# Probs times v in the column halves of the array, with v as the stationary operand

## The chip, the cores and the metric

The kernel runs on one core of one Trainium2 chip. The metric is the time of one launch on the device, in microseconds (us). The kernel before takes 615.45 us, the median of three runs (615.38 to 615.69).

## The reference

One layer of a hybrid decoder on 512 tokens of 1024 features, all in fp32. What the change touches is the attention of 8 heads of 64 features. With 512 tokens, blocks of 256 keys and a top-k that takes every past block, the block-sparse attention is plain causal attention. Its output is normalised over all 512 features of a token and goes, beside the output of a gated mixer, through the output projection:

```python
def rms_norm(x, g):
    y = xf * lax.rsqrt(jnp.mean(xf * xf, axis=-1, keepdims=True) + NORM_EPS)
...
    s_own = jnp.where(k_pos[None, None, :] <= q_pos[None, :, None], s_own, NEG_INF)
    probs = jax.nn.softmax(jnp.concatenate([s_sel, s_own], axis=-1), axis=-1)
    return (jnp.einsum('hqnl,hqnld->hqd', p_sel, v_sel)
            + jnp.einsum('hql,hld->hqd', p_own, v_own))
...
    mixed = jnp.concatenate([rms_norm(attn_out, attn_out_g[i]),
                             rms_norm(gmlp_out, gmlp_out_g[i])], axis=-1)
    h = h + rms_norm(jnp.einsum('bse,ed->bsd', mixed, w_o[i]), mix_post_g[i])
```

## The kernel before, in words

All matrices go through TensorE (PE). A large product is done as three fp32r matmuls of high and low parts (`product`, lines 1546, 1550, 1551), so every operand is split: ScalarE (ACT) writes the high part, VectorE (DVE) the low part. Tokens come in four tiles of 128. Each engine has its own instruction list, written out by hand; an instruction waits on semaphores, and all behind it on its engine wait with it.

The attention lies in a loop of 16 steps, one for each pair of heads of each tile of queries: `unit = 4 * qt + pair`. In a step PE does

- `scores(step)`: q times k for two heads, head 0 in rows 0 to 63 of the array and head 1 in rows 64 to 127, each into its own PSUM bank;
- `turn_probs(step - 1)`: transposes of the probabilities of the unit before, `qt + 1` for each head;
- `proj(...)`: half a tile of a projection, 4 slabs of weights times 3 matmuls. Steps 0 to 5 do the tiles 17 to 19 (v), steps 6 on those of the output projection (20 to 24);
- `attend(step - 1)`: probs times v (line 1698). The stationary operand is `probsT` (128 keys by 128 queries), the moving one 64 columns of `v`; the result is 128 queries by 64 features per head, so that bank 7 (`BANK_O`) holds attn by tokens. An fp32 matmul shows as two records in the trace: 80 matmuls, 160 records.

When the four pairs of a tile are done (after steps 4, 8, 12 and behind the loop), DVE takes 1/rowsum (line 557, 8 numbers a row) and multiplies it in (559), ACT squares with a sum over the row (924), POOL (GpSimd) makes the rstd (1327, 1328), DVE scales (566), PE turns attn by four transposes (`turn_attn`, in steps 5, 9, 13 behind `attend`), ACT drains the high part into `mixT_hi` and DVE the low part into `mixT_lo` (`attn_turn_hi`, `attn_turn_lo`). The second half of the first output tile of these tokens waits for that: `pe.wait_ge(*drained["attnT", t])`.

On DVE a step is `row_maxima(step)` (mask 536, maximum 541, times minus scale 544; it waits for `scores(step)`), `drain_pt0(step - 1)` (550, half of the transposed probs), then splits of weights in steps 0 to 2 and 5 to 8 (433), and what the attn chain needs. ACT does `drain_pt1` (1028), `softmax` (1019), the high parts of the same splits (890), and its part of the chain. `scores(step)` waits for `softmax(step - 1)`.

Behind the loop PE does `turn_probs(15)`, tile 25, the transposes of the hidden state (`turn_hn`), `turn_attn(3)`, tiles 26 and 27, then eight tiles for the per-layer embedding (`ple_tile`) with `turn_hn(4)` to `(7)` among them, and the MLP.

Of the kernel before, what the change touches and what calls it, by code (L numbers as in the profile page):

```python
# [32 lines left out]
F32 = mybir.dt.float32  # L33
F32R = mybir.dt.float32r
BF16 = mybir.dt.bfloat16
ALU = mybir.AluOpType
# [3 lines left out]
P = 128  # L40
D = 1024
SEQ = 512
TT = SEQ // P
# [70 lines left out]
def phase_one_results():  # L114

    names = []
    for n in range(20):
        names.append(("proj", n))  # L120
        if n in (8, 9):
            names += [("mix", 2 * (n - 8)), ("mix", 2 * (n - 8) + 1)]
        if 9 <= n <= 16:
            names.append(("qkT", n - 9))
        if 12 <= n <= 15:
            names.append(("gateT", n - 12))
    names += [("proj", n) for n in range(20, 26)]
# [6 lines left out]
    late = [(("attnT", 0), b), (("proj", 20), a), (("proj", 21), b), (("attnT", 1), c),  # L134
            (("proj", 22), c), (("proj", 23), a), (("attnT", 2), b), (("proj", 24), b),
            (("hT", 0), 5), (("hT", 1), 6), (("proj", 25), c), (("hT", 2), a), (("hT", 3), 6),
            (("attnT", 3), 5), (("proj", 26), 3), (("proj", 27), 4),
            (("ple", 0), 7), (("ple", 1), 6), (("ple", 2), 5), (("hT", 4), a), (("hT", 5), b),
            (("ple", 3), c), (("ple", 4), 7), (("ple", 5), 6), (("hT", 6), 3),
            (("hT", 7), 4), (("ple", 6), 5), (("ple", 7), a)]  # L140
    banks.update(late)
    return names[:-6] + [name for name, _ in late], banks
# [36 lines left out]
def hymba_layer(nc, x, xT, pT, weights, columns, rope, ws, rows, out):  # L179
# [6 lines left out]
    with ExitStack() as ctx:  # L186
# [34 lines left out]
        rinv = place("rinv", [P, HEADS])  # L221
        ident = place("ident", [P, P])
        ident_bf = place("ident_bf", [P, P], BF16)
        causal = place("causal", [P, P])
        stat = place("stat", [P, 114 + len(GATE_TILES)])
# [52 lines left out]
        minus_half = stat[:, 0:4]  # L278
        ss_x, rstd_x = stat[:, 4:8], stat[:, 8:12]
        ss_gm, rstd_gm = stat[:, 12:16], stat[:, 16:20]  # L280
        ss_at, rstd_at = stat[:, 20:24], stat[:, 24:28]
# [13 lines left out]
        def sem(name):  # L295
# [30 lines left out]
        rinv_ready, attn_ready, at_squared, at_rstd, at_scaled = (  # L326
            sem("rinv_ready"), sem("attn_ready"), sem("at_squared"), sem("at_rstd"), sem("at_scaled"))
# [90 lines left out]
        def _(dve):  # L418
# [134 lines left out]
            def attn_rows(qt):  # L553

                dve.wait_ge(pv_done, PAIRS * (qt + 1))
                sums = rowsum[:, PAIRS * qt:PAIRS * (qt + 1), :].rearrange("p a b -> p (a b)")
                nc.vector.reciprocal(rinv[:], sums).then_inc(rinv_ready, 1)
                dve.wait_ge(rinv_ready, qt + 1)
                nc.vector.tensor_tensor(attn[:].rearrange("p (h d) -> p h d", d=DH),
                                        psum[:, BANK_O, :].rearrange("p (h d) -> p h d", d=DH),  # L560
                                        rinv[:, :, None].to_broadcast([P, HEADS, DH]), ALU.mult
                                        ).then_inc(attn_ready, 1)

            def attn_scale(qt):
                dve.wait_ge(at_rstd, qt + 1)
                nc.vector.tensor_scalar(attn[:], attn[:], rstd_at[:, qt:qt + 1], None, ALU.mult
                                        ).then_inc(at_scaled, 1)

            def attn_turn_lo(qt):
                cut = slice(qt * P, (qt + 1) * P)  # L570
                turn_lo(("attnT", qt), mixT_lo[:, 4:8, cut], mixT_hi[:, 4:8, cut], bank1["attnT", qt])
# [27 lines left out]
            for step in range(TT * PAIRS):  # L599
                if step >= 6 and step % 4 == 2:  # L600
                    attn_turn_lo(step // 4 - 1)
                row_maxima(step)
                if step >= 1:
                    drain_pt0(step - 1)
                if step >= 5 and step % 4 == 1:
                    attn_scale(step // 4 - 1)
                for slab in STEP_SPLITS.get(step, ()):
                    splits(slab)
                if step >= 4 and step % 4 == 0:
                    attn_rows(step // 4 - 1)  # L610
# [4 lines left out]
            drain_pt0(15)  # L615
            hn_turn_lo(0)
            hn_turn_lo(1)
            attn_rows(3)
            attn_scale(3)
            hn_turn_lo(2)  # L620
            hn_turn_lo(3)
            attn_turn_lo(3)
# [256 lines left out]
        def _(act):  # L879
# [150 lines left out]

            def square_attn(qt):
                act.wait_ge(attn_ready, qt + 1)
                square(attn[:], ss_at[:, qt:qt + 1], at_squared)

            def attn_turn_hi(qt):
                turn_hi(filled1["attnT", qt], mixT_hi[:, 4:8, qt * P:(qt + 1) * P], bank1["attnT", qt])
# [8 lines left out]
            def square_h1(t):  # L1045
                act.wait_ge(*drained["proj", 21 + 2 * t])
                square(h[:, t, :], ss_h[:, t:t + 1], h1_squared)
# [16 lines left out]
            for step in range(TT * PAIRS):  # L1064
                if step >= 6 and step % 4 == 2:
                    attn_turn_hi(step // 4 - 1)
                if step >= 1:
                    drain_pt1(step - 1)
                softmax(step)
                for slab in STEP_SPLITS.get(step, ()):  # L1070
# [8 lines left out]
                if step >= 4 and step % 4 == 0:  # L1079
                    square_attn(step // 4 - 1)  # L1080
                if step == 14:
                    square_out(1)
# [4 lines left out]
            norm_h1(1)  # L1087
            square_attn(3)
# [4 lines left out]
            attn_turn_hi(3)  # L1093
# [204 lines left out]
        def _(pool):  # L1298
# [19 lines left out]
            pool.wait_ge(constants_set, 4)  # L1318
# [64 lines left out]
            def attn_rstd(qt):  # L1383
                pool.wait_ge(at_squared, qt + 1)
                rstd(rstd_at[:, qt:qt + 1], ss_at[:, qt:qt + 1], W, at_rstd)

# [5 lines left out]
            def hidden_rstd(t):  # L1392
                pool.wait_ge(h1_squared, t + 1)
                rstd(rstd_h[:, t:t + 1], ss_h[:, t:t + 1], D, h1_rstd)

# [144 lines left out]
        def _(pe):  # L1540
# [33 lines left out]
            def proj(n, k_range=range(KD)):  # L1574
# [17 lines left out]
                if half == 0 and k_range[-1] == KD - 1:  # L1592
                    pe.wait_ge(*drained["attnT", t])
# [37 lines left out]
            def turn_attn(qt):  # L1631
                pe.wait_ge(at_scaled, qt + 1)
                turn(phase1, bank1, ("attnT", qt), attn[:])
# [84 lines left out]
            turn_hn(1)  # L1718
            attend(15)
# [195 lines left out]
```

## Time and profile before

| | before |
|---|---|
| median of 3 runs | 615.45 us |
| the profiled execution | 615.13 us |
| its span | 613.4 us |
| PE busy | 603.8 us, 98% |
| DVE busy | 396.4 us, 65% |
| ACT busy | 311.0 us, 51% |
| POOL busy | 84.2 us, 14% |
| mean granted clock of PE | 0.997 of 2.4 GHz |

The profile is one execution. "Busy" of PE counts matmuls whose ends are modelled and overlap the next one's start; how fast a sequence runs is read from start to start. The attention steps lie between about 112 and 198 us.

### The profile page before, as it was taken

How to read it: one execution, taken by the hardware profiler on the slowest of the kernel's cores; microseconds unless marked ns; L12 is line 12 of the kernel's file. 1: busy time of each engine (PE TensorE's matmuls, PEld its weight loads, DVE VectorE, ACT ScalarE, POOL GpSimd, SP SyncE). 2: the span in 40 equal slices, each digit the busy share in tenths (PEclk: the TensorE clock that was granted, in tenths of full speed). 3: DMA queues.
4: the chain of work that ended last, by engine and by line, in shares of the span. 5: the costliest groups of instructions: out<-in, count | busy, mean ns of one | idle time of the engine just before them, and what ended most of it. 6: DMA issues, size and time to landing. Idle time of an engine off the chain costs nothing.

```text
span 613.4 us, 7770 instructions
## 1 busy us (share of the span) xinstructions
PE 603.8 (98%) x2910; PEld 499.5 (81%) x2910; DVE 396.4 (65%) x587; ACT 311.0 (51%) x541; POOL 84.2 (14%) x155
## 2 busy tenths in 40 slices
PE   8999999999999999999999999999999999999995
PEld 6888888888888888888888888888888888888884
DVE  5476443557545693765867857757668568568654
ACT  6754543655364755554544635545446345534422
POOL 1176332000001120001001001010010010001011
PEclk9999999999999999999999999999999999999998
DMA  8754322223000359564736546637365466234011
GB/s 309 258 189 141 105 103 69 69 69 104 1 2 1 111 202 313 141 218 92 191 138 152 157 138 153 219 79 196 144 128 156 151 154 207 96 130 171 10 70 68
DMA packets 23653, 82.90 MB, mean 135 GB/s; under 512 B 2752, under 2 KB 3136, under 8 KB 23104
## 3 DMA queue, kind: packets, MB, share of 16 engines
q1 hardware_dynamic: 18000, 60.83, 27.8%
q0 software_dynamic: 4032, 14.68, 13.5%
q10 hardware_dynamic: 1584, 6.90, 2.9%
q8 instruction: 23, 0.38, 0.2%
q14 instruction: 14, 0.11, 0.1%
HBM read 78.20 MB, written 4.19 MB: 134 GB/s over the span
## 4 chain that ended last, share of the span: by engine, by line
PE 97%; DMA 1%; DVE 0%; ACT 0%; SPq 0%; POOL 0%; issue 0%; DVEq 0%; ACTq 0%; POOLq 0%
PE psum L1546 30%; PE psum L1551 30%; PE psum L1550 30%; PE psum L1698 3%; PE psum L1600 2%; PE psum L1681 2%; DMA first_raw_a<-weights_dram 1%; PE psum L1614 1%; DVE h L829 0%; SPq L1461 0%; DVE w_lo L433 0%; ACT w_hi L890 0%; POOL stat L1445 0%; DVE acc L811 0%; DVE acc L802 0%
## 5 line engine op out<-in xcount | busy, mean ns | idle before, releaser
L433 DVE SCALAR_TENSOR_TENSOR w_lo<-raw,cols,w_hi 128x512 fp32r<-128x512 f32 x112 | 85.7, 808 | 48.8 <-ACT w_hi L890 48.8
L1551 PE MATMUL psum<-actT_hi,w_lo 128*128 128x512 f32 x256 | 99.8, 390 | 0.0
L1546 PE MATMUL psum<-actT_hi,w_hi 128*128 128x512 f32 x256 | 99.7, 389 | 0.0
L1550 PE MATMUL psum<-actT_lo,w_hi 128*128 128x512 f32 x256 | 99.6, 389 | 0.0
L890 ACT ACTIVATE w_hi<-raw,cols 128x512 fp32r<-128x512 f32 x112 | 74.3, 713 | 42.7 <-PE psum L1546 22.6
L1546 PE MATMUL psum<-w_hi,actT_hi 128*128 128x512 f32 (+1 forms) x232 | 90.7, 391 | 0.8 <-DVE w_lo L433 0.8
L1551 PE MATMUL psum<-w_hi,actT_lo 128*128 128x512 f32 (+1 forms) x232 | 88.9, 383 | 0.0
L1550 PE MATMUL psum<-w_lo,actT_hi 128*128 128x512 f32 (+1 forms) x232 | 88.7, 382 | 0.0
L1551 PE MATMUL psum<-t_hi,a_lo 128*128 128x512 f32 x212 | 83.6, 394 | 0.0
L1546 PE MATMUL psum<-t_hi,a_hi 128*128 128x512 f32 x212 | 83.5, 394 | 0.0
L1550 PE MATMUL psum<-t_lo,a_hi 128*128 128x512 f32 x212 | 83.4, 394 | 0.0
L719 DVE TENSOR_TENSOR acc<-acc,psum 128x512 f32<-128x512 f32 x90 | 58.5, 682 | 23.7 <-PE psum L1551 23.7
L1546 PEld LDWEIGHTS psum<-actT_hi,w_hi 128*128 128x128 f32 x256 | 48.1, 188 | 10.1
L1550 PEld LDWEIGHTS psum<-actT_lo,w_hi 128*128 128x128 f32 x256 | 48.1, 188 | 10.1
L1551 PEld LDWEIGHTS psum<-actT_hi,w_lo 128*128 128x128 f32 x256 | 48.1, 188 | 10.1
L1411 POOL DMA_DIRECT2D raw_x<-weights_dram x21 | 18.6, 885 | 259.1 <-DVE t_lo L660 259.1
L1546 PEld LDWEIGHTS psum<-w_hi,actT_hi 128*128 128x128 f32 x232 | 43.6, 188 | 9.9 <-DVE w_lo L433 1.2
L660 DVE TENSOR_TENSOR t_lo<-raw_x,t_hi 128x1024 fp32r<-128x1024 f32 x28 | 34.3, 1224 | 25.6 <-ACT t_hi L1136 25.5
L1551 PEld LDWEIGHTS psum<-w_hi,actT_lo 128*128 128x128 f32 x232 | 43.6, 188 | 8.6
L1550 PEld LDWEIGHTS psum<-w_lo,actT_hi 128*128 128x128 f32 x232 | 43.7, 188 | 7.9
L1136 ACT ACTIVATE t_hi<-raw_x 128x1024 fp32r<-128x1024 f32 x28 | 29.6, 1057 | 35.3 <-DMA raw_x<-weights_dram 25.8
L1550 PEld LDWEIGHTS psum<-t_lo,a_hi 128*128 128x128 f32 x212 | 39.8, 188 | 9.4
(157 smaller groups left out, 924.1 us busy)
## 6 DMA issues: line engine op xcount, KB each, us to landing
raw<-weights_dram SPq DMA_DIRECT2D x66, 512.0 KB, 3.5
raw_o<-weights_dram SPq DMA_DIRECT2D x23, 512.0 KB, 4.0
raw_x<-weights_dram POOLq DMA_DIRECT2D x21, 512.0 KB, 5.3
raw_x<-weights_dram SPq DMA_DIRECT2D x9, 512.0 KB, 5.1
raw_o<-weights_dram POOLq DMA_DIRECT2D x7, 512.0 KB, 8.9
ple_spill<-ple ACTq DMA_DIRECT2D x1, 2048.0 KB, 9.7
out_dram<-h SPq DMA_DIRECT2D x7, 256.0 KB, 2.0
xT_raw<-xT_dram SPq DMA_DIRECT2D x4, 256.0 KB, 5.3
```

Of the source, the lines that this page charges most:

```text
L433: nc.vector.scalar_tensor_tensor(out=w_lo[:, place_at, :], in0=source, scalar=gain, in1=high, op0=ALU.mult, op1=ALU.subtract).then_inc(sla ...
L660: nc.vector.tensor_tensor(t_lo[n % T_RING][:], t_source(n), t_hi[n % T_RING][:].bitcast(F32), ALU.subtract).then_inc(t_lo_done, 1)
L719: nc.vector.tensor_tensor(part, part, bank, how).then_inc(product_added, 1)
L890: nc.scalar.activation(w_hi[:, place_at, :], source, ACT.Copy, scale=gain).then_inc(slab_hi, 1)
L1136: nc.scalar.activation(t_hi[n % T_RING][:], t_source(n), ACT.Copy).then_inc(t_hi_done, 1)
L1411: nc.gpsimd.dma_start(raw_x[step % 2][:], weights[down_in_stream(step, rows, half)], accum_op=ALU.add).then_inc(x_added, 16)
L1546: begin = nc.tensor.matmul(out, a_hi, b_hi, start=first, stop=False, skip_group_check=read_between)
L1550: nc.tensor.matmul(out, a_hi, b_lo, start=False, stop=False, skip_group_check=read_between)
L1551: return nc.tensor.matmul(out, a_lo, b_hi, start=False, stop=last, skip_group_check=read_between)
L1600: mm = nc.tensor.transpose(psum[:, banks[name], j * P:(j + 1) * P], source[:, j * P:(j + 1) * P], ident[:])
L1681: mm = nc.tensor.transpose(psum[:, BANK_PT + s, k * P:(k + 1) * P], probs[:, unit % 2, s, k * P:(k + 1) * P], ident[:])
L1698: mm = nc.tensor.matmul(psum[:, BANK_O, head * DH:(head + 1) * DH], probsT[:, s, k, :], v[:, k, head * DH:(head + 1) * DH], start=(k == 0) ...
```

## The change

It exchanges the operands of probs times v. The 64 columns of `v` of a head become the stationary operand and `probsT` the moving one, 128 columns of it. The result is 64 features by 128 queries. Head 0 of a pair goes to PSUM partitions 0 to 63 and head 1 to 64 to 127, that is to the two column halves of the array, and the two alternate in the order. attn so comes out by features, and needs no transposes; but what was one number per row is now one per column:

- 1/rowsum is written by DVE over all 64 features of each head (`attn_inverse`, 128x512), turned by the four transposes that turned attn before (`turn_inverse`, now in steps 4, 8, 12 behind `turn_probs`), and drained by ACT to SBUF (`drain_inverse`); then DVE multiplies (`attn_columns`).
- The mean of the squares is over partitions: ACT squares, DVE adds the four pairs (`attn_sum`), a matmul with one moving column adds over partitions (`mean_square`), DVE adds epsilon (`attn_mean`), POOL takes the power (one instruction where there were two), DVE copies it over 128 columns (`attn_spread`), one transpose turns it (`turn_scale`), DVE scales (`attn_scale`).
- The high and low parts of attn now come from SBUF (`attn_hi`, `attn_lo`).

On PE, around step 4. The kernel before; `attn` doesn't occur yet, the rows with `v,probsT` are probs times v:

```order
L1681 MATMUL psum<-ident,probs 128x128 [waits probs_ready]
L1681 MATMUL psum<-ident,probs 128x128
L1546 MATMUL psum<-w_hi,actT_hi 128x512 [waits act_drained]
L1550 MATMUL psum<-w_lo,actT_hi 128x512
L1551 MATMUL psum<-w_hi,actT_lo 128x512
```

The same place after the change; L1750 are the transposes of the probabilities, L1657 those of the inverse:

```order
L1608 MATMUL psum<-kT_hi,mixT_lo 128x256
L1750 MATMUL psum<-ident,probs 128x128 [waits probs_ready]
L1750 MATMUL psum<-ident,probs 128x128
L1657 MATMUL psum<-ident,attn 128x128 [waits act_drained,rinv_ready]
L1657 MATMUL psum<-ident,attn 128x128 x3
L1603 MATMUL psum<-w_hi,actT_hi 128x512 [waits act_drained]
```

The four transposes stand two matmuls behind the scores of the same step, ahead of the projection; before they stood behind the attend of the next step.

On DVE, the same step after the change. The first row is the mask of `row_maxima(4)`:

```order
L541 TENSOR_TENSOR psum<-psum,causal 128x2x128 [waits scores_ready]
L546 TENSOR_REDUCE stat<-psum 128x2 [waits probs_ready,scores_masked]
L549 TENSOR_SCALAR stat<-stat 128x2 [waits max_found]
L555 COPY probsT<-psum 128x128 [waits pt_filled]
L562 RECIPROCAL attn<-rowsum 128x512 [waits probs_ready]
L569 TENSOR_TENSOR attn<-psum,attn 128x512 [waits inverse_drained,pv_done]
```

The reciprocal of 128x512 takes the place of one of 128x8, and stands behind a row that waits for this step's scores.

On DVE behind step 5 and in step 6 after the change:

```order
L574 TENSOR_REDUCE at_rows<-junk 128x128 [waits at_squared]
L438 SCALAR_TENSOR_TENSOR w_lo<-raw,cols,w_hi 128x512 [waits slab_hi] x2
L579 TENSOR_SCALAR stat<-psum 128x1 [waits mean_filled]
L584 COPY at_rows<-stat 128x128 [waits at_rstd]
L541 TENSOR_TENSOR psum<-psum,causal 128x2x128 [waits scores_ready]
L546 TENSOR_REDUCE stat<-psum 128x2 [waits probs_ready,scores_masked]
L549 TENSOR_SCALAR stat<-stat 128x2 [waits max_found]
L555 COPY probsT<-psum 128x256 [waits pt_filled]
L591 TENSOR_TENSOR attn<-attn,psum 128x512 [waits scale_filled]
L438 SCALAR_TENSOR_TENSOR w_lo<-raw,cols,w_hi 128x512 [waits slab_hi] x2
L598 TENSOR_TENSOR mixT_lo<-attn,mixT_hi 128x4x128 [waits turned_hi]
```

The low part of attn moved from the front of step 6 to its end, behind two splits.

The core of the diff:

```diff
-            def attn_rows(qt):
-                dve.wait_ge(pv_done, PAIRS * (qt + 1))
-                sums = rowsum[:, PAIRS * qt:PAIRS * (qt + 1), :].rearrange("p a b -> p (a b)")
-                nc.vector.reciprocal(rinv[:], sums).then_inc(rinv_ready, 1)
-                dve.wait_ge(rinv_ready, qt + 1)
-                nc.vector.tensor_tensor(attn[:].rearrange("p (h d) -> p h d", d=DH),
...
+            def attn_inverse(qt):
+                dve.wait_ge(probs_ready, PAIRS * (qt + 1))
+                sums = rowsum[:, PAIRS * qt:PAIRS * (qt + 1), :].rearrange("p a b -> p (a b)")
+                nc.vector.reciprocal(attn[:].rearrange("p (h d) -> p h d", d=DH),
+                                     sums[:, :, None].to_broadcast([P, HEADS, DH])).then_inc(rinv_ready, 1)
+            def attn_columns(qt):
+                dve.wait_ge(pv_done, PAIRS * (qt + 1))
+                dve.wait_ge(inverse_drained, qt + 1)
+                nc.vector.tensor_tensor(attn[:], psum[:, BANK_O, :], attn[:], ALU.mult).then_inc(attn_ready, 1)
+            def attn_sum(qt):
+                dve.wait_ge(at_squared, qt + 1)
+                nc.vector.tensor_reduce(at_rows[:], junk[:, W:2 * W].rearrange("p (a q) -> p q a", a=PAIRS),
+                                        AXIS_X, ALU.add).then_inc(at_summed, 1)
...
             for step in range(TT * PAIRS):
                 if step >= 6 and step % 4 == 2:
-                    attn_turn_lo(step // 4 - 1)
+                    attn_spread(step // 4 - 1)
                 row_maxima(step)
                 if step >= 1:
                     drain_pt0(step - 1)
+                if step >= 4 and step % 4 == 0:
+                    attn_inverse(step // 4 - 1)
...
+            def attn_hi(qt):
+                act.wait_ge(at_scaled, qt + 1)
+                nc.scalar.activation(mixT_hi[:, 4:8, qt * P:(qt + 1) * P],
+                                     attn[:].rearrange("p (a q) -> p a q", a=PAIRS), ACT.Copy
...
+            def mean_square(qt):
+                pe.wait_ge(at_summed, qt + 1)
+                nc.tensor.matmul(psum[:, BANK_O, W - P:W - P + 1], at_rows[:], mean_of_w[:],
+                                 start=True, stop=True).then_inc(mean_filled, 1)
+            def turn_scale(qt):
+                pe.wait_ge(at_spread, qt + 1)
+                nc.tensor.transpose(psum[:, BANK_O, W - P:W], at_rows[:], ident[:]
...
-                for s in range(2):
-                    head = 2 * pair + s
-                    pe.wait_ge((pt0_drained, pt1_drained)[s], unit + 1)
-                    for k in range(qt + 1):
-                        mm = nc.tensor.matmul(psum[:, BANK_O, head * DH:(head + 1) * DH],
-                                              probsT[:, s, k, :], v[:, k, head * DH:(head + 1) * DH],
+                if pair == 1 and qt:
+                    pe.wait_ge(at_scaled, qt)
+                pe.wait_ge(pt0_drained, unit + 1)
+                pe.wait_ge(pt1_drained, unit + 1)
+                for k in range(qt + 1):
+                    for s in range(2):
+                        head = 2 * pair + s
+                        mm = nc.tensor.matmul(psum[s * DH:(s + 1) * DH, BANK_O, pair * P:(pair + 1) * P],
+                                              v[:, k, head * DH:(head + 1) * DH], probsT[:, s, k, :],
                                               start=(k == 0), stop=(k == qt))
                 mm.then_inc(pv_done, 1)
...
+                if step in (4, 8, 12):
+                    turn_inverse(step // 4 - 1)
+                if step in (6, 10, 14):
+                    turn_scale(step // 4 - 1)
                 n, k0 = STEP_TILES[step]
                 proj(n, range(k0, k0 + 4))
                 if step >= 1:
                     attend(step - 1)
                 if step in (5, 9, 13):
-                    turn_attn(step // 4 - 1)
+                    mean_square(step // 4 - 1)
...
             turn_hn(0)
             turn_hn(1)
+            turn_inverse(3)
             attend(15)
             proj(25, range(4, 8))
             turn_hn(2)
             turn_hn(3)
-            turn_attn(3)
-            for part in (range(0, 4), range(4, KD)):
-                proj(26, part)
-                proj(27, part)
+            mean_square(3)
+            proj(26, range(0, 4))
+            turn_scale(3)
+            proj(27, range(0, 4))
+            proj(26, range(4, KD))
+            proj(27, range(4, KD))
```

## Rows read from the trace of the kernel before

**Rows 1.** Longest wait of PE behind its start: releaser, us in all, times, longest

```profile
PE psum L1546 <- DVE w_lo L433: 0.8, 2, 0.4
```

**Rows 2.** Timeline of PE in step 15: start us, length us, operation, count

```profile
183.16 1.90 PE L1698 MATMUL psum<-v,probsT 128*128 128x64 f32 x16
184.99 0.51 PE L1546 MATMUL psum<-kT_hi,mixT_hi 64*128 64x512 f32 x2
185.33 0.41 PE L1550 MATMUL psum<-kT_lo,mixT_hi 64*128 64x512 f32 x2
185.56 0.40 PE L1551 MATMUL psum<-kT_hi,mixT_lo 64*128 64x512 f32 x2
185.90 1.09 PE L1681 MATMUL psum<-ident,probs 128*128 128x128 f32 x8
186.75 0.48 PE L1546 MATMUL psum<-w_hi,mixT_hi 128*128 128x512 f32 x1
```

**Rows 3.** Timeline of PE around step 4

```profile
124.37 0.56 PE L1698 MATMUL psum<-v,probsT 128*128 128x64 f32 x4
124.86 0.39 PE L1546 MATMUL psum<-kT_hi,mixT_hi 64*128 64x256 f32 x2
125.61 0.49 PE L1546 MATMUL psum<-w_hi,actT_hi 128*128 128x512 f32 x1
```

**Rows 4.** Timeline of PE: gated mixer's matmuls with 256 moving columns

```profile
56.70 1.89 PE L1614 MATMUL psum<-gv,wsT 128*128 128x256 f32 x8
```

**Rows 5.** Timeline: DVE's drain and PE's next start, in steps 4, 8, 12

```profile
126.81 0.28 DVE L550 COPY probsT<-psum 128x128 f32<-128x128 f32 x1
...
144.83 0.48 PE L1546 MATMUL psum<-w_hi,mixT_hi 128*128 128x512 f32 x1
146.08 0.42 DVE L550 COPY probsT<-psum 128x256 f32<-128x256 f32 x1
...
167.48 0.48 PE L1546 MATMUL psum<-w_hi,mixT_hi 128*128 128x512 f32 x1
168.78 0.55 DVE L550 COPY probsT<-psum 128x384 f32<-128x384 f32 x1
```

**Rows 6.** Groups of DVE, shapes apart: busy us, mean ns, idle before

```profile
L550 DVE COPY probsT<-psum 128x512 f32<-128x512 f32 x4 | 2.7, 686 | 1.0 <-PE psum L1681 1.0
L544 DVE TENSOR_SCALAR stat<-stat 128x2 f32<-128x2 f32 x16 | 2.7, 170 | 0.6
L550 DVE COPY probsT<-psum 128x128 f32<-128x128 f32 x4 | 1.1, 284 | 0.0
L557 DVE RECIPROCAL rinv<-rowsum 128x8 f32<-128x8 f32 x4 | 0.8, 201 | 4.7 <-PE psum L1698 4.7
```

**Rows 7.** Timeline behind step 5: DVE's splits, PE's scores; group of POOL

```profile
132.98 1.42 DVE L433 SCALAR_TENSOR_TENSOR w_lo<-raw,cols,w_hi 128x512 fp32r<-128x512 f32 x2 [0.69 <-ACT w_hi L890]
134.18 0.39 PE L1546 MATMUL psum<-kT_hi,mixT_hi 64*128 64x256 f32 x2
...
L1328 POOL TENSOR_TENSOR stat<-stat 128x1 f32<-128x1 f32 x24 | 14.0, 585 | 2.0
```

**Rows 8.** Timeline behind the loop; last row a group of PE's weight loads

```profile
201.63 0.48 PE L1546 MATMUL psum<-w_hi,mixT_hi 128*128 128x512 f32 x1
202.01 0.61 ACT L912 ACTIVATE mixT_hi<-psum 128x512 fp32r<-128x512 f32 x1
209.45 1.22 DVE L627 TENSOR_TENSOR pT_lo<-pT_raw,pT_hi 128x1024 fp32r<-128x1024 f32 x1
212.64 0.39 PE L1546 MATMUL psum<-w_hi,pT_hi 128*128 128x512 f32 x1
...
L1600 PEld LDWEIGHTS psum<-ident,work 128*128 128x128 f32 x64 | 7.6, 140 | 1.8 <-ACT work L1056 0.4
```

**Rows 9.** Stretches at the end: us, busy (x) of PE, PEld, DVE, ACT, POOL; PEclk, DMA, GB/s

```profile
606.00:607.00 1.00, 0.21 (x2) 0.00 (x1) 0.42 (x1) 0.30 (x1) 0.00 (x0) 1.00 0.00 0
...
610.00:611.00 1.00, 0.00 (x0) 0.00 (x0) 0.79 (x2) 0.00 (x0) 0.00 (x0) 0.66 0.13 49
```

More of the change, by code:

```diff
@@ L140, in phase_one_results @@
             (("hT", 7), 4), (("ple", 6), 5), (("ple", 7), a)]
+    assert c == banks["proj", 19]
     banks.update(late)
-    return names[:-6] + [name for name, _ in late], banks
+    return names[:-7] + [name for name, _ in late], banks
 def tail_results():
@@ L325, in hymba_layer @@
                                                         sem("pt1_drained"), sem("pv_done"))
-        rinv_ready, attn_ready, at_squared, at_rstd, at_scaled = (
-            sem("rinv_ready"), sem("attn_ready"), sem("at_squared"), sem("at_rstd"), sem("at_scaled"))
+        rinv_ready, inverse_drained, attn_ready, at_squared, at_summed, mean_filled, mean_ready = (
+            sem("rinv_ready"), sem("inverse_drained"), sem("attn_ready"), sem("at_squared"), sem("at_summed"),
+            sem("mean_filled"), sem("mean_ready"))
+        at_rstd, at_spread, scale_filled, at_scaled = (sem("at_rstd"), sem("at_spread"), sem("scale_filled"),
+                                                       sem("at_scaled"))
         o_squared, o_rstd, o_normed = sem("o_squared"), sem("o_rstd"), sem("o_normed")
@@ new lines, in attn_mean, with attn_spread @@
+            def attn_mean(qt):
+                dve.wait_ge(mean_filled, qt + 1)
+                nc.vector.tensor_scalar(mean_at[:, qt:qt + 1], psum[:, BANK_O, W - P:W - P + 1], EPS, None,
+                                        ALU.add).then_inc(mean_ready, 1)
+            def attn_spread(qt):
+                dve.wait_ge(at_rstd, qt + 1)
+                nc.vector.tensor_copy(at_rows[:], rstd_at[:, qt:qt + 1].to_broadcast([P, P])).then_inc(at_spread, 1)
+            def attn_scale(qt):
+                dve.wait_ge(scale_filled, qt + 1)
+                by_pair = attn[:].rearrange("p (a q) -> p a q", a=PAIRS)
+                scale = psum[:, BANK_O, W - P:W]
+                nc.vector.tensor_tensor(by_pair, by_pair, scale[:, None, :].to_broadcast([P, PAIRS, P]),
+                                        ALU.mult).then_inc(at_scaled, 1)
@@ L573, in add_mixed, with attn_lo @@
+            def attn_lo(qt):
+                cut = slice(qt * P, (qt + 1) * P)
+                turned[0] += 1
+                dve.wait_ge(turned_hi, turned[0])
+                drained_by_dve(nc.vector.tensor_tensor(
+                    mixT_lo[:, 4:8, cut], attn[:].rearrange("p (a q) -> p a q", a=PAIRS),
+                    mixT_hi[:, 4:8, cut].bitcast(F32), ALU.subtract), ("attn_lo", qt))
             def add_mixed(t):
@@ L604, in _ @@
                     drain_pt0(step - 1)
+                if step >= 4 and step % 4 == 0:
+                    attn_inverse(step // 4 - 1)
                 if step >= 5 and step % 4 == 1:
+                    attn_sum(step // 4 - 1)
+                if step >= 6 and step % 4 == 2:
                     attn_scale(step // 4 - 1)
@@ L608, in _ @@
                     splits(slab)
+                if step >= 6 and step % 4 == 2:
+                    attn_lo(step // 4 - 1)
                 if step >= 4 and step % 4 == 0:
-                    attn_rows(step // 4 - 1)
+                    attn_columns(step // 4 - 1)
+                if step >= 5 and step % 4 == 1:
+                    attn_mean(step // 4 - 1)
                 if step == 11:
@@ L615, in _ @@
             drain_pt0(15)
+            attn_inverse(3)
             hn_turn_lo(0)
             hn_turn_lo(1)
-            attn_rows(3)
-            attn_scale(3)
+            attn_columns(3)
+            attn_sum(3)
+            attn_mean(3)
             hn_turn_lo(2)
             hn_turn_lo(3)
-            attn_turn_lo(3)
+            attn_spread(3)
+            attn_scale(3)
+            attn_lo(3)
             for i in range(2):
@@ L1069, in _ @@
                 softmax(step)
+                if step >= 6 and step % 4 == 2:
+                    attn_hi(step // 4 - 1)
                 for slab in STEP_SPLITS.get(step, ()):
@@ L1079, in _ @@
                 if step >= 4 and step % 4 == 0:
+                    drain_inverse(step // 4 - 1)
                     square_attn(step // 4 - 1)
@@ L1092, in _ @@
             hn_turn_hi(3)
-            attn_turn_hi(3)
+            attn_hi(3)
             square_out(2)
@@ L1629, in turn_hn, with turn_inverse @@
                 turn(phase1, bank1, ("hT", i), work[:, j, :])
-            def turn_attn(qt):
-                pe.wait_ge(at_scaled, qt + 1)
-                turn(phase1, bank1, ("attnT", qt), attn[:])
+            def turn_inverse(qt):
+                name = ("attnT", qt)
+                pe.wait_ge(rinv_ready, qt + 1)
+                turn(phase1, bank1, name, attn[:])
+            def mean_square(qt):
[5 more added lines that the diff above has]
+                nc.tensor.transpose(psum[:, BANK_O, W - P:W], at_rows[:], ident[:]
+                                    ).then_inc(scale_filled, 1)
             pe.wait_ge(constants_set, 2)
```

49 lines of the change are left out of this document (25 added, 24 removed).

## The prediction

> **What bounds the kernel now.** I read the list of waits first. Behind its start PE waited for another engine 0.8 us in all [rows 1]. So PE's own work sets the end: what leaves PE's list is won in full, what is added costs in full, and so does every wait that the change puts into that list. Then I read the timeline of the attention steps, start to start, since ends are modelled, and for each new wait the engine that it waits for.
>
> **Probs times v on PE.** Sixteen records take 183.16 to 184.99, 1.83 us [rows 2]; four take 0.49 [rows 3]. That is (1.83 - 0.49) / 12 = 0.112 us a record and 0.04 a group, and for all 160 records in 16 groups 18.5 us. Such a record streams only 64 columns, but its weights are 128 columns; eight transposes, with 128 of each, take 186.75 - 185.90 = 0.85, 0.107 each [rows 2]. With 128 moving columns and 64 of weights a record should not be dearer: records with 256 moving columns take at most 1.89 / 8 = 0.236 [rows 4], so 128 take at most 0.118. The change therefore gains nothing by the exchange alone; it gains if the two column halves run at once. The scores speak for that: two heads in the row halves, six matmuls of 512 columns, show as pairs of records with nearly the same start, 0.23 from pair to pair [rows 2], where a single full matmul takes the same 0.23. So I take 80 x 0.112 = 8.96 us as gained. Lower bound 0 (the halves take turns).
>
> **Price of going in and out of halves.** The scores' three pairs should take 3 x 0.23 = 0.69; start to start to the next kind it is 185.90 - 184.99 = 0.91 [rows 2]. So 0.22 lie inside a stay in row halves. A stay costs about that, plus an entry that I put at 0.1 from the 0.34 against 0.23 of the first pair; but leaving falls together with entering the scores' halves. I take 0.25 for each of 16 groups, 4.0 us; bounds 16 x 0.11 = 1.8 and 16 x 0.35 = 5.6. The Trainium skill (TensorEngine Tiling, Tiling Modes) says that changing the mode drains the engine and that tiles run in parallel; the 0.22 and the pairs agree with both, and it gives no price.
>
> **Other work on PE.** `turn_inverse` has the four transposes of `turn_attn`: 0. `mean_square`: four matmuls of two records, 4 x 0.224, and a leaving of the halves, 0.1 each: 1.3. `turn_scale`: four transposes at 0.107 and a change of kind: 0.5. PE's work in sum: -8.96 + 4.0 + 1.3 + 0.5 = -3.2 us.
>
> **The wait for the inverse.** In steps 4, 8 and 12 `turn_inverse` stands right behind `scores` and `turn_probs` of the same step. What it waits for, DVE's reciprocal, stands behind `row_maxima` of that step, which can begin only when the scores are done, and behind `drain_pt0`. Behind the waiting transposes are the projection, `attend` and the next scores: all of PE. Before, DVE's drain ended at 127.09 in step 4, and PE was through with the transposes of probs at 125.61: 1.48 us. In step 8 it is 146.50 against 144.83, 1.67; in step 12 169.33 against 167.48, 1.85 [rows 3, 5]. DVE had begun the mask as soon as the scores were there, so a faster PE doesn't change these. With 0.1 for the hand-over (an estimate) 5.3 us, and then comes the reciprocal itself, three times.
>
> How long is a reciprocal of 128x512? The copies give 284 ns for 128 elements and 686 for 512, that is 1.05 ns an element over 150 [rows 6]. At that rate it takes 0.69 us: the lower bound. But 8 elements took 201 ns where two of a plain operation take 170: (201 - 170) / 6 = 5.2 ns an element, or (201 - 150) / 8 = 6.4 over the copies' base. 512 of them are 2.8 or 3.4 us. I take 3.1. All 201 ns per element would be 201 / 8 x 512 = 12.9 us, an upper bound without weight, as the plain operation shows that most of the 201 is fixed. So the three waits are 5.3 + 3 x 3.1 = 14.6 us (at the lower bound 7.4). The Trainium skill (VectorE: DVE Perf Modes, First, the fixed hardware budget) says that reciprocal is iterated, with a repeat count of 8. Eight times the copies' step would be 4.4 us, an estimate, and the sum would be 3.9 us more; the row of 8 elements (150 + 67 = 217 against 201) does not quite bear it out. The fourth inverse is behind tile 25 and two groups of transposes and should be hidden.
>
> **Steps 6 and 7.** `turn_scale(0)` waits for DVE's `attn_spread`, and that for POOL's power and for `attn_mean`, which now stands behind the two splits of step 5. Those ended at 134.40, when scores(6) had started at 134.18 [rows 7]. From there 0.17 + 0.59 (POOL) + 0.28 and hand-overs: about 135.6. PE, half a microsecond ahead by then and through with scores and transposes in 1.0, gets there 0.8 earlier. Then in step 7 the second half of tile 20 needs the low part of attn, which DVE does behind the splits of step 6, and those follow ACT's high parts, which follow `attn_hi`: I count 1.2 us. In steps 9 to 15 there are no splits, and the chain fits under 2.8 us of projection. 2.0 us; bounds 0 and 4. Waits moved into `attend` (both halves of probsT, and `at_scaled`) I cost at 0: behind 2.8 us of projection.
>
> **Behind the loop.** ACT copied the high part of the last attn at 202.01, 0.4 after PE began tile 26 [rows 8]. Now it needs `turn_scale(3)`, issued behind half of tile 26 (12 matmuls of 0.23, 2.8 us), and 0.7 of scaling on DVE: about 205.2, 3.2 later, with `square_out(2)`, the splits and `norm_h1` queued behind it. The low part of p ended at 210.67 and was needed at 212.64 [rows 8], so 1.2 of the 3.2 come through there; and the transposes of the last hidden tile had already waited 0.4 for ACT [rows 8], so more comes through. I take 2.6 of 3.2; bounds 0 and 3.2.
>
> **Sum.** -3.2 + 14.6 + 2.0 + 2.6 = +16.0 on the profiled 615.13 (span 613.4 and 1.7 around it): 631.1. The median is 0.3 above that execution: 631.5 us. POOL loses an instruction per tile and DMA is not touched: 0.
>
> **Rivals.**
> - The reciprocal runs at the copies' rate. For it: nothing but that 201 ns is one small row. Against: both readings of that row. Then 3 x (3.1 - 0.69) = 7.2 less: 624.3 us.
> - The column halves take turns. For it: the scores' halves read different rows of SBUF, here both halves stream all 128 partitions, in fp32. Against: nothing in the rows. 9.0 more: 640.5.
> - PE's clock falls in the new waits. It was full at 606 to 607, where PE's last work ended, and 0.66 in the mean over 610 to 611, so it fell to 1.2 GHz near 610.3, some 4 us after the work [rows 9]. The new waits are 4.7, 4.9 and 5.1 us. At 1.2 GHz each microsecond costs a half; if it stays low for 4 us each time, 6 more: 637.5. The Trainium skill (TensorE: Matmul & The Clock Gate, Why this matters for your kernels) says that idle gaps between bursts of matmuls bring the lower clock back; the end of this trace fits it.
> - The other side, faster than before: the work saved outweighs the waits. PE saves at most 8.96 - 1.8 - 1.8 = 5.4 us, so it decides once the new waits are under 5.4 in all. It asks for an inverse at the copies' rate and, in each of steps 4, 8 and 12, over half a microsecond less than the rows show ahead of it, and for nothing in steps 6 and 7 or behind the loop. At 3.2 saved and no waits left: 612.2.
>
> **Chances.** Forecast 0.45 (its own range 628 to 635), ordinary reciprocal 0.17, halves in turns 0.10, clock 0.22, faster 0.03, and 0.03 for what I don't see, of which 0.02 near no change. A measurement of this kernel tells 0.2% (1.2 us). Faster 0.03, same 0.02, slower 0.95. Range 622 to 641.
>
> **What would show it.** In the new profile: the transposes of `attn` waiting three times for DVE's reciprocal, 4.7 to 5.1 us each; the reciprocal's mean at about 3100 ns; probs times v with two records per 0.11 us, groups of 16 in about 1.1 us; small waits of the scale's transpose in step 6 and of the tile in step 7; PE's clock at 1.00 in all three waits. If the reciprocal's group shows 700 ns, or there is no wait at those transposes, the forecast is wrong; if a group of 16 still takes 1.8 us, the gain is.

## The result, and the profile after

| | kernel before | changed kernel |
|---|---|---|
| median, us | 615.57 (615.38 to 615.81, 4 runs) | 636.51 (635.34 to 637.14, 4 runs) |
| profiled execution: its time, span | 615.13, 613.4 | 637.14, 635.4 |

The ratio is 1.0338 (95% interval 1.032 to 1.0356): the kernel became 3.4% slower. Of the cases in the prediction the one that came is the forecast together with its third rival: the three waits are there, and PE's clock falls in or just behind them. The range (622 to 641) holds the time, the forecast's own range (628 to 635) doesn't. The predicted 631.5 is 5.0 too low, which is the clock's doing.

Where PE waits, changed kernel (releaser; us in all, times, longest). It answers to [rows 1]:

```profile
PE psum L1657 <- DVE attn L562: 14.2, 3, 4.9
...
PE psum L1657 <- ACT work L1109: 1.5, 1, 1.5
PE psum L1603 <- issue: 1.4, 1, 1.4
PE psum L1603 <- DVE w_lo L438: 0.9, 2, 0.6
PE psum L1603 <- DVE mixT_lo L598: 0.7, 1, 0.7
PE psum L1701 <- DVE at_rows L584: 0.3, 1, 0.3
```

The first row is `turn_inverse` in steps 4, 8 and 12. The wait of 1.4 for which the profile names no releaser ("issue") ends at 232.86, 0.1 after DVE has finished the low part of p at 232.76. DVE's groups of the attention part, shapes apart (busy us, mean ns), which answer to [rows 6]:

```profile
L562 DVE RECIPROCAL attn<-rowsum 128x512 f32<-128x512 f32 x4 | 13.4, 3342 | 0.0
L574 DVE TENSOR_REDUCE at_rows<-junk 128x128 f32<-128x512 f32 x4 | 4.3, 1069 | 0.7 <-ACT junk L1082 0.7
```

One reciprocal of 512 elements takes 3.34 us, (3342 - 150) / 512 = 6.2 ns an element, where a copy takes 1.05. The timeline of PE through step 4 and the two other waits (start us, length us; in brackets the wait), which answers to [rows 3]:

```profile
124.39 0.44 PE L1770 MATMUL psum<-probsT,v 128*64 128x128 f32 x4
124.76 0.39 PE L1603 MATMUL psum<-kT_hi,mixT_hi 64*128 64x256 f32 x2
...
125.32 0.44 PE L1750 MATMUL psum<-ident,probs 128*128 128x128 f32 x2
130.31 1.12 PE L1657 MATMUL psum<-ident,attn 128*128 128x128 f32 x4 [4.55 <-DVE attn L562]
131.08 0.78 PE L1603 MATMUL psum<-w_hi,actT_hi 128*128 128x512 f32 x1
131.65 0.63 PE L1607 MATMUL psum<-w_lo,actT_hi 128*128 128x512 f32 x1
132.08 0.63 PE L1608 MATMUL psum<-w_hi,actT_lo 128*128 128x512 f32 x1
...
152.59 0.66 PE L1750 MATMUL psum<-ident,probs 128*128 128x128 f32 x4
157.98 1.11 PE L1657 MATMUL psum<-ident,attn 128*128 128x128 f32 x4 [4.74 <-DVE attn L562]
...
180.94 0.87 PE L1750 MATMUL psum<-ident,probs 128*128 128x128 f32 x6
186.73 0.95 PE L1657 MATMUL psum<-ident,attn 128*128 128x128 f32 x4 [4.92 <-DVE attn L562]
```

Start to start the projection's matmuls are 132.08 - 131.65 = 0.43 us apart, where [rows 2] have 0.23 for 512 columns. The granted clock says why. Stretches of the changed kernel (us; busy and count of PE, PEld, DVE, ACT, POOL; granted clock as a share of 2.4 GHz; DMA share, GB/s), for the first and the third wait:

```profile
127.00:128.00 1.00, 0.00 (x0) 0.00 (x0) 1.00 (x1) 0.86 (x4) 0.00 (x0) 1.00 0.00 0
128.00:129.00 1.00, 0.00 (x0) 0.00 (x0) 1.00 (x1) 0.00 (x0) 0.00 (x0) 0.96 0.00 0
129.00:130.00 1.00, 0.00 (x0) 0.00 (x0) 1.00 (x1) 0.00 (x0) 0.00 (x0) 0.50 0.00 0
...
134.00:135.00 1.00, 1.00 (x3) 0.78 (x3) 0.00 (x0) 0.00 (x0) 0.00 (x0) 0.50 0.00 0
135.00:136.00 1.00, 1.00 (x4) 0.65 (x2) 0.00 (x0) 0.00 (x0) 0.00 (x0) 0.63 0.00 0
136.00:137.00 1.00, 1.00 (x12) 0.62 (x10) 0.34 (x1) 0.00 (x0) 0.00 (x0) 1.00 0.00 0
...
186.00:187.00 1.00, 0.27 (x2) 0.27 (x3) 0.67 (x1) 0.51 (x1) 0.45 (x1) 0.97 0.00 0
187.00:188.00 1.00, 1.00 (x6) 0.90 (x5) 0.00 (x0) 0.92 (x2) 0.00 (x0) 0.50 0.00 0
...
190.00:191.00 1.00, 1.00 (x5) 0.83 (x4) 0.00 (x0) 0.00 (x0) 0.00 (x0) 0.82 0.00 0
```

The first row is PE idle at the full clock. The clock is at 1.2 GHz (0.50) from about 129.0 to 135.7, of which PE works from 130.3 on. In the second place it is low from 156.2 to 163.0, in the third from 187.0 to 190.4. In the third the clock falls 0.2 us after PE has begun again. If work at half the clock takes twice as long, half of this time is lost: (135.7 - 130.3) / 2 + (163.0 - 158.0) / 2 + (190.4 - 187.0) / 2 = 6.9 us, an estimate.

Probs times v in groups of 12 and of 16, and what PE does next, which answers to [rows 2]:

```profile
174.10 0.88 PE L1770 MATMUL psum<-probsT,v 128*64 128x128 f32 x12
174.91 0.45 PE L1603 MATMUL psum<-kT_hi,mixT_hi 64*128 64x384 f32 x2
...
203.27 1.09 PE L1770 MATMUL psum<-probsT,v 128*64 128x128 f32 x16
204.30 0.50 PE L1603 MATMUL psum<-kT_hi,mixT_hi 64*128 64x512 f32 x2
```

Sixteen records take 1.03 us to the next kind, against 1.83 before: the column halves do run at once, at (1.03 - 0.37) / 12 = 0.055 us a record, where the group of 4 takes 0.37 (124.76 - 124.39 above).

### The profile page after: what moved, and what is told of

It reads as the page before. It is cut to its first block, busy times and chain, and to the rows that moved or that the text cites. A ratio compares the mean times of both kernels' runs of the same rounds, so it can differ in the third digit from the quotient of the medians.

```text
span 635.4 us, 7818 instructions
## 1 busy us (share of the span) xinstructions
PE 607.6 (96%) x2922; PEld 494.4 (78%) x2922; DVE 413.6 (65%) x599; ACT 313.5 (49%) x541; POOL 82.7 (13%) x152
## 4 chain that ended last, share of the span: by engine, by line
PE 90%; DVE 5%; ACT 2%; issue 1%; DMA 1%; POOL 1%; SPq 0%; DVEq 0%; ACTq 0%; POOLq 0%
PE psum L1603 28%; PE psum L1608 28%; PE psum L1607 28%; PE psum L1657 2%; PE psum L1770 2%; DVE attn L562 2%; PE psum L1750 1%; DMA first_raw_a<-weights_dram 1%; DVE stat L546 1%; PE psum L1671 1%; ACT w_hi L931 0%; DVE w_lo L438 0%; DVE psum L611 0%; DVE w_lo L435 0%; DVE h L619 0%
## 5 line engine op out<-in xcount | busy, mean ns | idle before, releaser
L1468 POOL DMA_DIRECT2D raw_x<-weights_dram x21 | 18.5, 883 | 259.1 <-DVE t_lo L701 259.1
```

Of the source, the lines that this page charges most:

```text
L1468: nc.gpsimd.dma_start(raw_x[step % 2][:], weights[down_in_stream(step, rows, half)], accum_op=ALU.add).then_inc(x_added, 16)
```

## The experiments

The ratios are to the kernel before, with their 95% intervals. The theory at this point: three waits for a long reciprocal, and a clock that falls in them.

**The reciprocal alone.**

```diff
-                nc.vector.reciprocal(attn[:].rearrange("p (h d) -> p h d", d=DH),
-                                     sums[:, :, None].to_broadcast([P, HEADS, DH])).then_inc(rinv_ready, 1)
+                nc.vector.reciprocal(rinv[:], sums).then_inc(rinv_small, 1)
+                dve.wait_ge(rinv_small, qt + 1)
+                nc.vector.tensor_copy(attn[:].rearrange("p (h d) -> p h d", d=DH),
+                                      rinv[:, :, None].to_broadcast([P, HEADS, DH])).then_inc(rinv_ready, 1)
```

> The changed kernel, but the reciprocal is taken of the 8 row sums (as before the change) and then copied over the 64 features of each head. Theory: the three waits of the inverse's transposes, 4.55, 4.74 and 4.92 us, are mostly the 3.34 us reciprocal, and they are long enough for PE's clock to fall. With 0.2 + 0.7 us in its place they are about 2.1, 2.3 and 2.5, the clock stays at 1.00, and the time is 636.5 - 7.3 - 6.6 = 622.6 us. Rival (the clock falls for the half-array matmuls, not for the gaps): 629 us, with the clock low as now. Rival (the place in the order is all, a later link ends last anyway): over 633 us.

627.17 us (624.42 to 628.58, 4 runs), ratio 1.0186 (1.0155 to 1.0218). The broadcast copy takes 0.43 us and the reciprocal 0.19, and the three waits sum to 6.1: the reciprocal is worth 8.1 us of waiting. But the time stayed 4.6 above what was expected. The clock had fallen here too, behind waits of only 1.86 and 2.05 us, and not behind the third, of 2.23. PE's timeline, and the stretches behind the first and the third wait:

```profile
128.53 0.70 PE L1661 MATMUL psum<-ident,attn 128*128 128x128 f32 x4 [1.86 <-DVE attn L566]
...
152.59 0.85 PE L1661 MATMUL psum<-ident,attn 128*128 128x128 f32 x4 [2.05 <-DVE attn L566]
...
177.83 0.66 PE L1661 MATMUL psum<-ident,attn 128*128 128x128 f32 x4 [2.23 <-DVE attn L566]
```

```profile
128.00:129.00 1.00, 0.47 (x5) 0.47 (x5) 0.44 (x2) 0.77 (x4) 0.00 (x0) 1.00 0.00 0
129.00:130.00 1.00, 1.00 (x5) 0.81 (x4) 0.00 (x0) 0.60 (x1) 0.00 (x0) 0.51 0.00 0
...
132.00:133.00 1.00, 1.00 (x5) 0.80 (x4) 0.00 (x0) 0.00 (x0) 0.00 (x0) 0.79 0.00 0
...
179.00:180.00 1.00, 1.00 (x6) 0.80 (x5) 0.00 (x0) 0.27 (x2) 0.49 (x2) 1.00 0.00 0
```

The first fall comes when PE is already at work again, half a microsecond behind the wait, and the second 0.3 behind it. The clock stays low for some 3.4 us each time, a loss of 1.7 each, 3.4 of the 4.6; the rest isn't placed. The executions scatter by 4 us, about two such falls; the mean clock of the execution of 624.42 was 0.994, that of the profiled one, 627.12, 0.991.

**The place alone.** The transposes of the inverse move behind the projection and `attend`; the reciprocal stays long.

```diff
-                if step in (4, 8, 12):
-                    turn_inverse(step // 4 - 1)
...
                 if step >= 1:
                     attend(step - 1)
+                if step in (4, 8, 12):
+                    turn_inverse(step // 4 - 1)
```

> The changed kernel, with only the inverse's transposes of steps 4, 8 and 12 moved from behind the transposes of probs to behind that step's attend. Theory: 2.8 us of projection and the attend now cover the wait; the long reciprocal still ends some 1.5 us later than PE arrives, so three waits of about 1.5 us stay, the clock stays full: 636.5 - 14.2 - 6.6 + 4.5 = 620.2 us. If the product on DVE, now held up by the later drain, delays the next step's row maxima enough to reach PE: up to 3 us more. Rival (place matters little): over 630 us.

621.52 us (621.41 to 621.89, 4 runs), ratio 1.0103 (1.0086 to 1.0119): 1.3 above what was expected, within its margin. PE's longest wait, and three stretches with the places in question:

```profile
PE psum L1657 <- DVE attn L562: 4.2, 3, 1.4
```

```profile
126.00:136.00 10.00, 8.55 (x54) 6.34 (x54) 8.01 (x12) 4.90 (x15) 0.00 (x0) 1.00 0.01 2
146.00:160.00 14.00, 12.61 (x90) 9.18 (x88) 11.55 (x16) 6.71 (x16) 0.42 (x1) 1.00 0.21 76
172.00:190.00 18.00, 16.66 (x123) 12.46 (x122) 12.44 (x19) 10.52 (x24) 1.77 (x6) 1.00 0.00 1
```

Some 3 us of each wait are covered, and behind waits of 1.4 us the clock stays full. The move gives 15.0 us where the waits that it covers are 10.0. The rest is the clock, less 1.6 for two waits that grew (`w_lo` 0.9 to 1.8, `at_rows` 0.3 to 1.0).

**Filling the wait with matmuls.** The work and the waits stay as changed; ahead of the wait PE multiplies 128 columns of a bfloat16 identity, results unused, first 36 times.

```diff
+                if qt < 3:
+                    bank_free(phase1, bank1, name)
+                    for _ in range(FILL_MATMULS):
+                        nc.tensor.matmul(psum[:, bank1[name], 0:P], ident_bf[:], ident_bf[:], start=True, stop=True)
                 pe.wait_ge(rinv_ready, qt + 1)
```

> The changed kernel, with 36 bf16 matmuls of 128 columns issued by PE in each of the three gaps, before it waits for the inverse; they write the bank that the transposes then overwrite. The wait ends when it ended before, so only the clock can change. Theory: the low clock after the gaps costs 6.6 us; kept at 1.00, the time is 630 us. Rival (the low clock comes from the half-array matmuls or is only shown and costs nothing): 636 us. If the 36 matmuls take longer than the gap, each microsecond over it adds three.

635.42 us (634.96 to 636.06, 4 runs), ratio 1.0325 (1.0308 to 1.0342). It doesn't price the clock, and the expected 630 was missed: 36 matmuls took only 2.17 us, gaps of 2.54 to 2.9 were left, and the clock fell all the same (0.988 in the mean), three times for 3.4 us. The same with 74:

> As the kernel with the filled gap, with 74 bf16 matmuls instead of 36 (these took 2.17 us and left gaps of 2.5 to 2.9 us, in which the clock fell all the same). 74 take 4.5 us, so that the gaps are at most 0.5 us. Theory: the clock stays at 1.00 and the time is 636.5 - 6.6 = 630 us with the inverse ready when it was. Rival (the low clock isn't tied to the gaps): clock low in the same places and 635 us or more.

631.07 us (630.69 to 634.58, 4 runs), ratio 1.0275 (1.025 to 1.0301): 1.1 above what was expected. The timeline and the stretch to be laid beside those of the changed kernel:

```profile
130.35 0.66 PE L1658 MATMUL psum<-ident,attn 128*128 128x128 f32 x4 [0.42 <-DVE attn L563]
```

```profile
130.00:135.00 5.00, 4.65 (x29) 3.55 (x30) 1.09 (x3) 0.67 (x2) 0.00 (x0) 1.00 0.01 3
```

In step 4 the inverse arrives at the same moment, 130.35 against 130.31, so nothing of the wait's length was saved; what follows runs at the full clock. The matmuls in column halves are the same as in the changed kernel, so it isn't they that bring the clock down. The span is 629.1 against 635.4, so the clock's price is 6.3 us (by the medians 5.4), in line with the 6.9 summed up from the stretches.

**The column halves.** The matmuls of one head follow each other, instead of alternating with those of the other head, which sits in the other column half.

```diff
-                for k in range(qt + 1):
-                    for s in range(2):
+                for s in range(2):
+                    for k in range(qt + 1):
```

> The changed kernel, with the matmuls of probs times v issued head after head instead of alternating between the column halves. Theory (PE starts what its halves allow, as it does with the scores, which are also issued head after head): a group of 16 records stays at 1.03 us and the time within 0.5 us of 636.5. Rival (strict order, only neighbours overlap): a group of 16 takes nearly 1.8 us, and all groups about 5 to 7 us more: 642 us.

640.23 us (638.89 to 640.97, 4 runs), ratio 1.0402 (1.0385 to 1.042), 3.7 above the changed kernel. Neither theory as it stood: groups of 4 and 8 records kept their 0.37 and 0.59 us, 12 took 1.07 for 0.81, 16 took 1.51:

```profile
204.87 1.58 PE L1770 MATMUL psum<-probsT,v 128*64 128x128 f32 x16
206.38 0.50 PE L1603 MATMUL psum<-kT_hi,mixT_hi 64*128 64x512 f32 x2
```

By the groups that is 4 x (0.26 + 0.48) = 3.0 us. With up to four records (two matmuls) of one head in a row the halves overlap as before; with eight records (four matmuls) in a row only in part.

**Both repairs.** Short reciprocal with broadcast copy, and the transposes behind `attend`.

> The changed kernel with both: reciprocal of the 8 row sums copied over the features, and the inverse's transposes behind attend. Theory: the inverse is ready before PE gets there, no wait at these transposes, PE's clock at 1.00, and of the 21 us only the small waits (about 4: steps 6 and 7, and 2.9 behind the loop) less PE's saved work (2.7) stay: 616.5 us, with little scatter. Rival (the exchange itself costs PE time, hidden so far in my balance): over 618 us, with PE not waiting.

619.23 us (619.09 to 620.04, 5 runs), ratio 1.0065 (1.0051 to 1.0078). The wait for the inverse is gone, but a new one stands in an attend, for DVE's drain of the transposed probs (1.3), and that for `at_rows` grew from 0.3 to 0.9. The time is 2.7 above what was expected, of which these explain 1.9; the rest isn't placed. It lies where the rival put it (over 618), but the rival's condition, PE not waiting, isn't met.

**The other waits.** On top of it, `square_out(2)` goes ahead of `attn_hi(3)` on ACT, the low part of attn ahead of the splits on DVE, and the scale's transpose behind half a tile (steps 6, 10, 14) or three slabs (behind the loop).

```diff
-            attn_hi(3)
             square_out(2)
+            attn_hi(3)
...
+                n, k0 = STEP_TILES[step]
                 if step in (6, 10, 14):
+                    proj(n, range(k0, k0 + 2))
                     turn_scale(step // 4 - 1)
-                n, k0 = STEP_TILES[step]
-                proj(n, range(k0, k0 + 4))
+                    proj(n, range(k0 + 2, k0 + 4))
```

> As the kernel with both, and the small waits attacked: behind the loop ACT squares the output tile before it waits for the last attn, and the scale's transpose stands behind 3 slabs of tile 26 instead of 4; in steps 6, 10, 14 the scale's transpose stands behind two slabs of the projection, and in step 6 DVE does the low part of attn before the splits. Theory: the 2.9 us behind the loop fall to about 0.5, the 1.7 of steps 6 and 7 to nearly 0: 612.5 us, faster than the kernel before by the work saved on PE. Rival (the waits move on to the splits and to the next row maxima): 615 us or more.

615.64 us (615.05 to 616.01, 11 runs), ratio 1.0004 (0.9995 to 1.0013): no change from before, and 3.1 above what was expected: the time of its rival. The attend's wait of 1.3 is still there. The timeline in step 12 shows its cause:

```profile
174.08 0.69 DVE L573 TENSOR_TENSOR attn<-psum,attn 128x512 f32<-128x512 f32 x1 [4.60 <-ACT attn L1078]
```

DVE's product, with the mask, the maxima and the drain queued behind it, waits for ACT's drain of the transposed inverse, and that stood behind `norm_h1(0)`, issued just ahead of it.

**ACT's order.** `drain_inverse` goes ahead of `norm_h1(0)` in step 12, and, behind the loop, `square_out(3)` ahead of `norm_h1(2)`.

```diff
                     square_h1(0)
-                    norm_h1(0)
                 if step >= 4 and step % 4 == 0:
                     drain_inverse(step // 4 - 1)
+                if step == 12:
+                    norm_h1(0)
+                if step >= 4 and step % 4 == 0:
                     square_attn(step // 4 - 1)
```

> As the kernel with the small waits attacked (615.6 us), with two more turns in ACT's order: in step 12 the drain of the inverse stands ahead of the norm of the first hidden tile (ACT waited there for POOL, and the product on DVE, the next row maxima and an attend of PE waited 1.3 us in the end), and the squares of the last output tile stand ahead of the third hidden tile's norm (PE waited 1.4 us for the last hidden tile). Theory: both waits go, and the work saved on PE, about 3 us, begins to show: 613.2 us, faster than before by 0.3%. Rival (each wait removed is followed by the next one of the chain): 615 us or more.

613.36 us (612.9 to 614.01, 6 runs), ratio 0.9966 (0.9954 to 0.9978): as expected, and faster than both kernels. All of PE's waits:

```profile
PE psum L1609 <- DVE w_lo L440: 1.7, 2, 1.3
PE psum L1714 <- POOL ident_bf L1372: 1.6, 1, 1.6
PE psum L1663 <- ACT work L1113: 0.4, 1, 0.4
PE psum L1776 <- DVE attn L595: 0.2, 1, 0.2
```

From 120 to 230 us PE is busy for 109.3 of 110.

**Two controls.** The reorder on ACT behind the loop could have helped the kernel before as well, so the gain might not be the change's:

```diff
-            norm_h1(2)
             square_out(3)
+            norm_h1(2)
```

> A control: the kernel before, with only the squares of the last output tile ahead of the third hidden tile's norm on ACT. PE waited there 0.4 us at most. Theory: 0 to 0.4 us faster, 615.2 us, so that what the repaired kernel wins beyond that is the change's. Rival (this order was a loss all along): 614.4 us or less.

615.26 us (614.67 to 615.57, 11 runs), ratio 0.9998 (0.9989 to 1.0007): it gives nothing there. The other changes of order weren't tried in the kernel before; there PE waits 0.8 us in all behind its start [rows 1], less than the 1.9 gained. And the halves' overlap priced where no wait can swallow it, in the repaired kernel with head after head:

> As the repaired kernel, with the matmuls of probs times v issued head after head. With PE bound nearly everywhere the loss shows in full. Theory: the groups of 4, 8, 12 and 16 records take what they took in the unrepaired kernel in that order (16 records 1.51 us against 1.03), about 4 us over all 16 groups: 617.2 us. Rival (part of it hides in waits): under 615.5 us.

616.18 us (615.84 to 617.01, 11 runs), ratio 1.0013 (1.0004 to 1.0023), 1.0 below what was expected. A group of 16 in each, the alternating order first:

```profile
176.29 1.09 PE L1776 MATMUL psum<-probsT,v 128*64 128x128 f32 x16
```

```profile
176.82 1.58 PE L1776 MATMUL psum<-probsT,v 128*64 128x128 f32 x16
```

The alternation is worth 2.8 us, more than the repaired kernel's whole gain over before (1.9).

## Why the prediction was right or wrong

**The waits for the inverse: right.** Counted 4.7, 4.9 and 5.1, in the list of waits 4.55, 4.74 and 4.92; 14.2 for 14.6. The list counts from the modelled end of the matmul before, the prediction from start to start. In the kernel before, the transposes of probs of these steps began here, and the next matmul at 125.61, 144.83 and 167.48 [rows 3, 5]:

```profile
125.42 0.44 PE L1681 MATMUL psum<-ident,probs 128*128 128x128 f32 x2
...
144.42 0.66 PE L1681 MATMUL psum<-ident,probs 128*128 128x128 f32 x4
...
166.85 0.87 PE L1681 MATMUL psum<-ident,probs 128*128 128x128 f32 x6
```

So the waits cost (130.31 - 125.32) - 0.19 = 4.80, 5.39 - 0.41 = 4.98 and 5.79 - 0.63 = 5.16, 14.9 in all. Of these the reciprocals are 3 x 3.34 = 10.0 (9.3 taken), which leaves 4.9 for what lies ahead of them (5.3 counted): two small misses that partly cancel. The short form bears the split out: by the list it saves 8.1, and 3 x (3.34 - 0.19 - 0.43) = 8.2. The reciprocal took 3.34 us, inside the 2.8 to 3.4 that the row of 8 elements gave; of its two readings the second, over the copies' base, was the better. The Trainium skill (VectorE: DVE Perf Modes, First, the fixed hardware budget) says that reciprocal runs with a repeat count of 8; the trace has 6.2 / 1.05, six times the copies' step.

**PE's clock: the step that failed.** The prediction said that the clock would be at 1.00 in all three waits. It left the clock out of the sum, as a rival with 0.22. Of [rows 9] it had read that the fall came some 4 us after the work; by that reading too waits of 4.7 to 5.1 are long enough, and no reason is given why the clock should have stayed up. The runs show that far less will do: the clock fell behind waits of 1.86 and 2.05 us in one kernel, and behind every one of 2.5 us or more. What [rows 9] show is one fall at the end of the program, where no work followed, and it says nothing on the least gap. The size came out near, 6 counted and 6.3 measured, but by some luck: it had a low clock of 4 us each time, and PE was at work under it for 5.4, 5.0 and 3.4. Against the profiled execution the sum was 6.0 low (631.1 for 637.14): 6.3 of clock, and all other terms together 0.3 too high. With the clock's 6 it gives 637.5, 1.0 above the median. That the range held the time is owed to the rivals that it had to cover. The Trainium skill (TensorE: Matmul & The Clock Gate, Why this matters for your kernels) warns of idle gaps between bursts of matmuls; the stretches at 0.50 agree, and the runs show falls behind shorter gaps than it names.

**PE's own work: right within a microsecond.** Of the span's +22.0, PE's new waits are 14.2 + 1.5 + 1.4 + 0.7 + 0.3 + 0.1 = 18.2 and the clock 6.3, which leaves -2.5, or -3.2 with the three waits at 14.9. The kernel with the transposes moved leaves +6.5 - 9.8 = -3.3, the repaired one -1.3 - 1.5 = -2.8. Predicted was -3.2. Its terms for probs times v: the groups take 4 x (0.37 + 0.59 + 0.81 + 1.03) = 11.2 for 18.5, 7.3 less, and the entry, from the last start of the projection to the first of the group, 0.32 for 0.23, 1.4 more in 16 groups; together -5.9, where the prediction had -8.96 + 4.0 = -5.0. By the record that is 160 x (0.112 - 0.055) = 9.1 saved, and 3.2 for going in and out of the halves. With the 1.3 and 0.5 of its other work the pieces give -4.1, a somewhat larger gain than the balance shows; that microsecond isn't placed.

**The halves side by side: right.** A pair of records in 0.11 us, a group of 16 in 1.03 for the 1.1 named.

**Steps 6 and 7: oversized.** 0.3 + 0.7 = 1.0 for 2.0, inside the bounds; each wait is half a microsecond shorter than counted. (For step 6 the prediction's own times give 135.6 - 134.7 = 0.9, not 0.8.)

**Behind the loop: right.** 1.5 + 1.4 = 2.9 for 2.6; that the delay comes through nearly whole was the right reading of [rows 8].

**The other rivals.** The ordinary rate of the reciprocal and the halves in turns are refuted by the rows above. The faster side asked for the waits to be gone; the experiments built that by hand, and got 1.9 us under before (613.36 against 615.27), with 1.5 us more of waits than before still in it, where the prediction gave 612.2 for no waits at all, 3.2 under.

The change lost mainly for two reasons of placing and form, and the repaired kernel shows that they aren't in the exchange itself: a broadcast reciprocal that computes 512 inverses for 8, and transposes issued right behind the scores on which that inverse hangs. Together they cost 14.2 us of waiting and 6.3 of clock, and the smaller new waits another 4.0, for some 3 us of saved matmul time.

## What to carry to other kernels

Where the tensor engine has no idle time, an added wait of some 2 us or more should be costed with a fall of its clock (here waits up to 1.5 us brought none, those of 1.9 to 2.2 two in three, those of 2.5 and more always; 1.7 us for a fall behind a short wait, 6.3 us for three behind long ones). Put independent matmuls ahead of the wait first. Invert before broadcasting: the reciprocal took 3.34 us for 512 elements a row and 0.19 for 8, and the broadcast copy 0.43. A two-head layout in column halves paid here only with the two heads' matmuls alternating in the order of issue.

## What the runs showed of the hardware that was not expected

- PE's clock fell behind idle gaps of 1.86, 2.05, 2.5 to 2.9 and 4.6 to 4.9 us, and not behind those of 1.3 to 1.5, nor behind one of 2.23. So the gap's length alone doesn't decide it; what else does is open. The traces of the changed kernel, of the short reciprocal, of the 36 filling matmuls and of head after head show eleven falls at these waits. In six it fell 0.2 to 0.9 us after work had begun again.
- It stayed at 1.2 GHz for 3.4 us in seven of the eleven, and for 6.8 us in the four where PE stayed idle for another 1.0 to 1.8 us after the fall.
- DVE's reciprocal takes 6.2 ns an element of a row (128x512 in 3.34 us, 128x8 in 0.19 to 0.20), a copy 1.05.
- Column halves of the array overlap for alternating matmuls (0.055 us a record, 0.11 a pair, for 0.112 a record before), and with head after head as well up to four records of a head in a row, in part for six (1.07 us for 0.81) and eight (1.51 for 1.03).
- Entering the column halves costs some 0.09 us more than entering a full matmul (0.32 for 0.23; 0.1 counted), and a whole stay some 0.2 (3.2 / 16; 0.25 counted).
